# Adding expert results to the tokens' sums on chip, item by item, instead of through DRAM

## What is computed

```python
logits = x2d @ w_router + b_router
top_vals, top_idx = lax.top_k(logits, 4)
gates = softmax(top_vals)
# for each expert e and each token that has chosen it:
gu = xb @ w_gate_up[e] + b_gate_up[e]
g, u = minimum(gu[:, :D_FF], 7), clip(gu[:, D_FF:], -7, 7)
hid = (u + 1.0) * (g * sigmoid(1.702 * g))
out = (hid @ w_down[e] + b_down[e]) * gate
y = zeros((n, D)).at[row_tok].add(out)
x = layer_norm(DEEPNORM_ALPHA * x + y, ln2_g, ln2_b)
```

## Time and profile before

| what | us |
|---|---|
| median of 3 runs | 1552.32 (1551.21 to 1552.47) |
| span of the profiled execution | 1546.4 |
| PE busy | 1282.3 (83%) |
| DVE busy | 347.7 (22%) |
| ACT busy | 260.4 (17%) |
| POOL busy | 70.2 (5%) |
| PE, gate and up (L1536, 2112 instructions) | 478.8 |
| PE, down (L1552, 1056 instructions) | 277.3 |

### The profile page before, as it was taken

How to read it: one execution, slowest core, us unless ns; L and a number is a source line. 1 busy time by engine, 2 the same in 40 slices (tenths; PEclk the granted TensorE clock), 3 DMA queues, 4 the chain that set the end, 5 groups by cost and what they waited for, 6 DMA issues and landing times.

```text
span 1546.4 us, 19222 instructions
## 1 busy us (share of the span) xinstructions
PE 1282.3 (83%) x6721; PEld 512.7 (33%) x6722; DVE 347.7 (22%) x661; ACT 260.4 (17%) x439; POOL 70.2 (5%) x104
## 2 busy tenths in 40 slices
PE   8997787875696989988899888899888878887875
PEld 3444554553444322322223222233222222222222
DVE  0003546465554010012101100100100010001006
ACT  0003556565321011010000000000000000000000
POOL 0000000000000000000000000000000000000003
PEclk9999899996595999989899999999999999999997
DMA  9055898997113999999999999799999999999965
GB/s 388 23 191 175 254 325 299 346 349 309 42 66 146 373 418 418 417 416 418 418 418 416 418 418 419 286 417 416 418 418 418 416 417 418 419 417 416 418 278 170
DMA packets 127322, 526.65 MB, mean 341 GB/s; under 512 B 14720, under 2 KB 14848, under 8 KB 93344
## 3 DMA queue, kind: packets, MB, share of 16 engines
q1 hardware_dynamic: 116080, 496.95, 80.3%
q0 software_dynamic: 5936, 20.71, 4.1%
q10 hardware_dynamic: 5280, 8.65, 1.5%
HBM read 507.39 MB, written 18.87 MB: 340 GB/s over the span
## 4 chain that ended last, share of the span: by engine, by line
PE 32%; DMA 16%; SPq 12%; DVE 5%; issue 2%; ACT 1%; POOL 0%; ACTq 0%; POOLq 0%
DMA arena<-in_w_gate_up 15%; PE psum L1536 15%; PE psum L1552 12%; SPq L225 12%; PE psum L1527 2%; PE psum L1542 1%; DVE arena L1639 1%; DVE arena L1635 1%; DVE arena L1631 1%; DVE arena L1632 1%; ACT arena L1597 1%; PE psum L1572 1%; PE psum L1427 0%; PE psum L1584 0%; SPq L1461 0%
## 5 line engine op out<-in xcount | busy, mean ns | idle before, releaser
L1536 PE MATMUL psum<-arena 128*64 128x512 f32 x2112 | 478.8, 601 | 33.1 <-DMA arena<-in_w_gate_up 33.0
L1552 PE MATMUL psum<-arena 128*64 128x512 f32 x1056 | 277.3, 685 | 22.6 <-ACT arena L1597 22.6
L1536 PEld LDWEIGHTS psum<-arena 128*64 128x64 f32 x2112 | 143.7, 138 | 367.5 <-issue 270.9
L1631 DVE TENSOR_SCALAR arena<-psum 128x512 f32<-128x512 f32 x33 | 22.8, 692 | 864.5 <-PE psum L1536 864.5
L1552 PEld LDWEIGHTS psum<-arena 128*64 128x64 f32 x1056 | 82.6, 157 | 197.6 <-issue 164.5
L1595 ACT ACTIVATE arena<-arena 128x512 f32<-128x512 f32 x33 | 20.8, 630 | 570.9 <-DVE arena L1631 570.9
L599 PE MATMUL psum<-arena 128*128 128x128 f32 x512 | 75.3, 287 | 25.7 <-DMA arena<-in_cache_sb_k 8.2
L1542 PE MATMUL psum<-arena 128*128 128x128 f32 x132 | 25.4, 323 | 74.6 <-DVE arena L1639 74.6
L282 PE MATMUL psum<-arena 128*128 128x512 f32 x192 | 85.8, 603 | 0.0
L506 ACT ACTIVATE arena<-psum 128x512 f32<-128x512 f32 x112 | 61.9, 574 | 82.2 <-PE psum L599 50.1
L599 PEld LDWEIGHTS psum<-arena 128*128 128x128 f32 x512 | 56.3, 144 | 41.3 <-issue 15.0
(11 more groups left out here) (192 smaller groups left out, 856.5 us busy)
## 6 DMA issues: line engine op xcount, KB each, us to landing
arena<-in_w_gate_up SPq DMA_DIRECT2D x256, 1024.0 KB, 20.2
arena<-in_w_down SPq DMA_DIRECT2D x128, 1024.0 KB, 23.2
arena<-in_cache_sb_k SPq DMA_DIRECT2D x64, 256.0 KB, 4.4
arena<-in_cache_diff_k SPq DMA_DIRECT2D x64, 256.0 KB, 8.2
arena<-in_cache_sb_v SPq DMA_DIRECT2D x64, 256.0 KB, 5.1
arena<-in_cache_diff_v SPq DMA_DIRECT2D x64, 256.0 KB, 6.7
arena<-in_w_in SPq DMA_DIRECT2D x8, 1536.0 KB, 20.4
expert_rows<-arena ACTq DMA_DIRECT2D x66, 128.0 KB, 6.1
```

Of the source, the lines that this page charges most:

```text
L1536: ins = nc.tensor.matmul(psum[64 * h:64 * h + 64, n, :], x_k, slot[k][:, col:col + 512], start=False, stop=(k == KD - 1))
L1552: ins = nc.tensor.matmul(psum[64 * h:64 * h + 64, 4, :], h_k, slot[s][:, col:col + 512], start=(k == 0), stop=(k == KD - 1))
L1631: nc.vector.tensor_scalar(gate_in, psum[:, 0, :], LIMIT, None, ALU.min).then_inc(gate_clamped, 1)
```

## The change

The table now gives 2 x token + 2, and 0 for an unused slot. At the end of each item DVE builds `scatter`, a 0/1 matrix of 128 slots (64 twice) by 320 tokens. One item later TensorE multiplies it with `y_rows` (`scatter_rows`: two matmuls for each block, one for each half of 64 rows, into two PSUM banks), and DVE multiplies the result with the item's gate for each token and adds it to `base` (`drain`). `base` starts as DEEP times x1 by three ScalarE copies. `turn(t + 1)` is moved behind the down matmuls, because the drained banks include bank 2. `y_dram`, its stores, its zero fill, the final gathers and the combining matmuls are gone. The first item stands ahead of the loop. The diff, cut to its core:

```diff
-    put("half", i // 64)
+    put("tokens", 2 * np.arange(TOKENS)[None, :] + 2)
+    put("half", i // 64 - 2)
...
-                pool.dma_start(y_dram[EXPERTS * SLOTS:, :].rearrange("(i s) d -> s i d", s=SLOTS),
-                               zeros[0:SLOTS, :].rearrange("p (o d) -> p o d", o=1).to_broadcast([SLOTS, MAX_EXTRA, D])
-                               ).then_inc(rows_zeroed, 16)
...
+                link.mark(nc.vector.tensor_copy(slot_token, psum[:, 2, 0:TABLE_ITEMS]))
...
+        PART = ((5, 6), (7, 2), (0, 1))
...
-                for b in order:
-                    nt = BLOCKS[b][1]
-                    for k in range(TOP_K):
-                        pool.indirect_dma_start(picks[0:nt, 4 * b + k, :], None, y_dram, bass.IndirectOffsetOnAxis(
-                            ap=place_y[0:nt, b, k:k + 1], axis=0)).then_inc(picked_up[b], 16)
...
             def _(pe):
+                def scatter_rows(b):
+                    t0, nt = BLOCKS[b]
+                    for h in range(2):
+                        r = slice(64 * h, 64 * h + 64)
+                        ins = nc.tensor.matmul(psum[0:nt, PART[b][h], :], scatter[r, t0:t0 + nt], y_rows[r, :],
+                                               start=True, stop=True)
+                    ins.then_inc(combined, 1)
...
                     pe.wait_ge(xg_copied, t + 1)
+                    if not first:
+                        pe.wait_ge(drained, 3 * t + (SEED - 3))
                     loaded = pe.value_load(started_i[0:1, bass.ds(t, 1)], min_val=16, max_val=16 * EXPERTS)
...
-                    turn(t + 1)
+                    if not first:
+                        pe.wait_ge(y_copied, t)
+                        pe.wait_ge(scatter_ready, t)
+                        scatter_rows(0)
+                        scatter_rows(1)
                     pe.wait_ge(hid_ready, t + 1)
                     for c in range(4):
                         ins = nc.tensor.transpose(psum[:, 3, c * P:(c + 1) * P], hid[:, c * P:(c + 1) * P], ident)
                     ins.then_inc(hid_turned, 1)
+                    if not first:
+                        scatter_rows(2)
                     pe.wait_ge(hid_copied, t + 1)
...
+                    if not first:
+                        pe.wait_ge(drained, 3 * t + (SEED - 1))
+                    turn(t + 1)
...
+                    pe.wait_ge(base_ready, 6)
+                for b in range(3):
+                    scatter_rows(b)
...
             def _(act):
+                for b in range(3):
+                    nt = BLOCKS[b][1]
+                    nc.scalar.activation(base[0:nt, b, :], x1[0:nt, b, :], ACT.Copy, scale=DEEP).then_inc(base_set, 1)
...
-                    act.wait_ge(y_stored, 32 * t + SEED)
+                    if not first:
+                        act.wait_ge(combined, 3 * t + SEED)
                     nc.scalar.activation(y_rows, psum[:, 4, :], ACT.Copy).then_inc(y_copied, 1)
-                    act.wait_ge(y_copied, t + 1)
-                    for h in range(2):
-                        act.dma_start(y_dram[bass.ds(t * SLOTS, SLOTS), h * 512:(h + 1) * 512],
-                                      y_rows[64 * h:64 * h + 64, :]).then_inc(y_stored, 16)
...
+                def drain(b, col):
+                    nt = BLOCKS[b][1]
+                    banks = PART[b]
+                    at_once = 2 if banks[1] == banks[0] + 1 else 1
+                    for h in range(0, 2, at_once):
+                        r = base[0:nt, b, h * 512:(h + at_once) * 512].rearrange("p (h d) -> p h d", h=at_once)
+                        ins = nc.vector.scalar_tensor_tensor(out=r, in0=psum[0:nt, banks[h]:banks[h] + at_once, :],
+                                                             scalar=item_gate[0:nt, b, col], in1=r,
+                                                             op0=ALU.mult, op1=ALU.add)
+                    return ins
...
                     nc.vector.tensor_tensor(hid, up_in, sig, ALU.mult).then_inc(hid_ready, 1)
+                    if first:
+                        dve.wait_ge(base_set, 3)
+                    else:
+                        for b in range(3):
+                            dve.wait_ge(combined, 3 * t + (b + SEED - 2))
+                            if b == 0:
+                                dve.wait_ge(drained, 3 * t + (SEED - 3))
+                            drain(b, bass.ds(t - 1, 1)).then_inc(drained, 1)
+                    nc.vector.tensor_scalar(scatter, const["tokens"], slot_token[:, bass.ds(t, 1)], None, ALU.is_equal
+                                            ).then_inc(scatter_ready, 1)
                     copy_x(t + 1)
...
-                            link.link(nc.vector.tensor_tensor(r[:, cols_], r[:, cols_], psum[:, COMBINED_BANK[b] + c, :], ALU.add))
...
+                        if c == 0:
+                            dve.wait_ge(combined, 3 * extras + (3 * EXPERTS + b + SEED - 2))
+                            link.link(drain(b, bass.ds(extras + (EXPERTS - 1), 1)))
```

More of the change, by code:

```diff
@@ L81, in constants @@
     put("slot", j % SLOTS)
-    put("token2", 2 * (i + np.array([[b[0] for b in BLOCKS]])))
-    put("half", i // 64)
+    put("token2", 2 * (i + np.array([[b[0] for b in BLOCKS]])) + 2)
+    put("tokens", 2 * np.arange(TOKENS)[None, :] + 2)
+    put("half", i // 64 - 2)
     put("is_c0", c == 0)
@@ L1389, in _ @@
                 dve.wait_ge(table_done, 1)
[L1390 to L1397, removed]
+                link.mark(nc.vector.tensor_scalar(idx_all, psum[:, 2, 0:TABLE_ITEMS], const["half"], 0.0, ALU.add, ALU.max))
+                link.mark(nc.vector.tensor_copy(slot_token, psum[:, 2, 0:TABLE_ITEMS]))
                 dve.wait_ge(col_turned, 1)
@@ L1432, in items @@
             extras = eng.value_load(count_i[0:1, 0:1], min_val=0, max_val=MAX_EXTRA)
+            body(0, first=True)
             if midway is None:
-                with eng.Fori(0, EXPERTS) as t:
+                with eng.Fori(1, EXPERTS) as t:
                     body(t)
             else:
-                with eng.Fori(0, EXPERTS // 4) as t:
+                with eng.Fori(1, EXPERTS // 4) as t:
                     body(t)
@@ L1574, in bias, with body @@
                                              ).then_inc(bias_done, 1)
[L1575 to L1587, removed]
+                    pe.wait_ge(base_ready, 6)
+                extras = items(pe, body, bias)
+                pe.wait_ge(drained, 3 * extras + (3 * EXPERTS + SEED - 3))
+                pe.wait_ge(y_copied, extras + EXPERTS)
+                pe.wait_ge(scatter_ready, extras + EXPERTS)
+                pe.wait_ge(xg_copied, extras + (EXPERTS + 1))
+                for b in range(3):
+                    scatter_rows(b)
             @block.scalar
             def _(act):
-                act.sem_inc(y_stored, SEED)
-                def body(t):
+                for b in range(3):
+                    nt = BLOCKS[b][1]
+                    nc.scalar.activation(base[0:nt, b, :], x1[0:nt, b, :], ACT.Copy, scale=DEEP).then_inc(base_set, 1)
+                def body(t, first=False):
                     act.wait_ge(gate_clamped, t + 1)
@@ L1620, in _ @@
             def _(dve):
+                dve.sem_inc(drained, SEED)
                 nc.vector.memset(ones_row[0:1, :], 1.0).then_inc(ones_ready, 1)
+                link = Count(dve, dve_link)
+                link.n = links[0]
                 def copy_x(t):
@@ L1625, in copy_x, with body @@
                     nc.vector.tensor_copy(xgT, psum[:, 2, :]).then_inc(xg_copied, 1)
-                copy_x(0)
-                def body(t):
+                def drain(b, col):
[8 more added lines that the diff above has]
+                    return ins
+                copy_x(0)
+                for b in order:
+                    nt = BLOCKS[b][1]
+                    link.link(nc.vector.reciprocal(norm_cols[0:nt, 32 + b:33 + b], norm_cols[0:nt, 28 + b:29 + b]))
+                    link.link(nc.vector.tensor_scalar(gates[0:nt, b, :], gates[0:nt, b, :],
+                                                      norm_cols[0:nt, 32 + b:33 + b], None, ALU.mult))
+                    for k in range(TOP_K):
+                        link.mark(nc.vector.tensor_scalar(gate_tmp[0:nt, k, :], const["slot"][0:nt, 0:TABLE_ITEMS],
+                                                          places[0:nt, 1, b, k:k + 1], gates[0:nt, b, k:k + 1],
+                                                          ALU.is_equal, ALU.mult))
+                    link.wait()
+                    link.link(nc.vector.tensor_reduce(item_gate[0:nt, b, :], gate_tmp[0:nt].rearrange("p k i -> p i k"),
+                                                      AX.X, ALU.add))
+                def body(t, first=False):
                     dve.wait_ge(w_used[KD - 1], t + 1)
@@ L1659, in residuals @@
                             link.link(ins)
[L1660 to L1663, removed]
                     dve.sem_inc(weight_ready, 1)
```

(11 more changed lines are left out.)

71 lines of the change are left out of this document (25 added, 46 removed).

## The result

The changed kernel takes 1577.6 us (median of four runs, 1577.1 to 1579.5) against 1551.8 us for the kernel before (four runs): ratio 1.0179, 95% interval 1.0163 to 1.0195 (these two medians alone divide to 1.0167). It is 1.8% slower. The forecast said 3.7% slower, 1610 us, in a range of 1550 to 1635. The direction and the mechanism came out, and the time lies in the range; the size of the loss was over-stated by more than a factor of two. The profiled execution spans 1577.5 us.

What follows compares the result with a forecast made beforehand. Weight loading was taken as the present bound, TensorE as the next at 32.5 us an item. Loop +75, tail -15 and zero fill -2.7 turn span 1546.4 into 1604; plus 5.9 gives 1610 us, range 1550 to 1635.

Steps and rivals of the forecast that it cites:

- the stores' saving: Stores of expert rows in the loop: removing 31 saves 19.4 us, if loading stays the bound.
- the hand-over: From the late turn behind down to the next item's bias: turn, copy and register load add 2.2 us an item.
- The rival with a clock that holds at the hand-over: In the loop, the clock stays full between items: period 29.8 us, 1526 us in all, chance 0.14.
- The tail: From the last down's end to the kernel's end: 42.7 us becomes 27.7, a gain of 15 us.
- midway part beyond an item: The loop's midway part costs about 11 us more than an item, as in the kernel before.
- the clock's price: At bias and early gate/up, the clock falls to half in nearly each item: 2.7 us an item (1.3 to 3.4).
- rival B: In the loop, the clock falls in under half the items or for a shorter time: 1562 us, chance 0.14.
- +0.5 for scatter_rows(2): Behind the transposes of hid, the third block's scatter matmuls outlast ScalarE's copy: 0.5 us an item (0.2 to 1.05).
- rival D: In the scatter matmuls, the two row halves don't overlap: 1.05 us more a period, 1644 us, chance 0.04.
- the 0.5 an item that was weighed: Array shape changes on TensorE's path: three drains might add 0.5 us an item, 16 us in all; taken as 0.
- the zero fill: Fill of 4864 KB beside the page loads: removing it saves one TensorE wait, 2.7 us (0 to 5).
- the 5.9 us between span and median: Whole kernel: the timed median lies 5.9 us above the profiled span, added to the forecast span of 1604.

## Why the prediction was right and wrong

Right: TensorE became the bound and the stores' saving was not to be had; the hand-over cost 2.21 us; the one-row bias did not hold the clock; the row halves overlapped (eight instructions in 1.99 us, which DVE's work on `hid` covers); DVE's drains cost the path nothing; the clock held in down, but for the first item. The rival with a clock that holds at the hand-over forecast 1526 us; made real by the 128-row bias it takes 1513.

```profile
1030.29 1.99 PE L1505 MATMUL psum<-arena 64*128 64x512 f32 x8
```

The tail, down's end to the end of the span, was 1577.5 - 1549.9 = 27.6 us, forecast 27.7:

```profile
1549.91 0.60 PE psum L1497 x4
...
1574.13 0.68 DVE arena L1128
```

Too large was the sum. Its terms, against the profiled execution (span 1604 forecast, 1577.5 measured):

| term | forecast us | measured us | difference |
|---|---|---|---|
| start of the first item's bias | 494.9 | 485.4 | -9.5 |
| first item | 30.4 | 32.2 | +1.8 |
| 32 items, full clock | 32 x 29.8 | 32 x 29.57 | -7.4 |
| 32 items, clock lost | 32 x 2.7 | 32 x 2.17 | -17.0 |
| midway part beyond an item | 11 | 16.7 | +5.7 |
| tail | 27.7 | 27.6 | -0.1 |

The 16.7 are down's end to the next bias at the midway part, 757.0 - 738.1 = 18.9, less the 2.2 of the hand-over, which every item has. The 2.17 are what 32 items take, (1549.9 - 517.6 - 16.7)/32 = 31.74, less the 29.57 of the item at the full clock. The first item has no scatter yet, and its down part met the low clock (8.78 us), which is its +1.8.

The failing step is the clock's price, "I take 2.7 (1.3 to 3.4)", and in it the reason "whose pattern is exactly the new one": the first item's price was taken to hold for nearly every item. In the kernel before, the clock of the first item is low from 498.2 to 505.0, 6.8 us, and that costs 3.4 us. In the changed kernel nine of the 32 items repeat this and lose 3.35 us (19.19 instead of 15.84 for bias and gate/up). One loses nothing, the one behind the midway part 4.3, and the other 21 are at the low clock for 3.4 us only and lose 1.7. The mean is 2.2. The price of 1.7 stood in rival B, "for the shorter time seen". The range had this, the chosen value did not, and with 32 items each tenth counts 3.2 us. In the full clock's period stood +0.5 for scatter_rows(2); the chain shows gate/up's end to down's start at 34.87 - 30.39 = 4.48 instead of 4.16, so +0.3. The stated range also leaves out rival D (1644 us), which the prediction's account of it does not say.

On switching array shapes: scatter_rows(2), 64-row matmuls behind 128-row transposes, takes 1.01 us for four instructions, where overlapped halves at gate/up's pace would take 0.87:

```profile
1033.21 0.66 PE psum L1543 x4
1033.87 1.01 PE psum L1505 x4
```

The Trainium skill, TensorEngine Tiling (Array Packing), Key Properties, says that a change of tiling mode drains TensorE. The trace does not contradict it, but all that it could cost at this place is in these 0.14 us. The undisturbed item, 29.57 us, is the 27.02 of before plus 0.32 here and 2.21 at the hand-over, to within 0.02, so the 0.5 an item that was weighed are not there. One other place, the same in both kernels, may pay: behind a one-row bias gate/up takes 13.91 us at the full clock, behind a 128-row bias 13.75. Whether these 0.16 us come from the change of shape no run isolates.

The second miss is the zero fill: 2.7 taken, range 0 to 5, 12 to 13 measured. The step read the one wait behind the fill and not the eight others of the same kind; all nine take 8.2 us in the kernel before. The first item of the changed kernel begins 12.1 us earlier than before (485.42 instead of 497.57), so some 4 us more came with them:

```profile
485.42 3.28 PE L1524 MATMUL psum<-arena 1*64 1x512 f32 x8 [1.45 <-DVE arena L1631]
```

Third, with the other sign: "the midway part costs about 11 us, as now". Its weights were hidden under down before; moving the turn moved DVE's copy, and with it the weights. I had asked who waits for copy_x in the loop but not at the loop's seam. Last, the 5.9 us between span and median were too much: the median of the changed kernel is 0.1 us above the profiled span. That execution took 1579.5 us in all, 2.0 above its span, so 5.9 held mostly the spread between executions. With it the forecast is 32.4 us too high: 26.5 in the span, of which the clock's price is 17.0, and 5.8 here.

## What to carry to other kernels

When an operation is moved to the seam of a loop, count the whole hand-over there, the sequencer's register loads behind the wait included, and ask what the queue used to run ahead of; here 2.2 us in 32 items and the clock lost with it outweighed 46 us of savings (stores 18, zero fill 13, tail 15). When TensorE has only a few us an item to spare, look at what fills each stretch without wide matmuls: a 2.2 us wait that was moved next to thin matmuls cost 2.2 us of clock on top. A loss seen once is not the loss of each item: look whether it comes in more than one size, and how often each. Where TensorE waits for loads again and again, price a removed transfer by its bytes (11.9 us estimated and 13 measured, 19.4 and 18.0), not by the one wait that follows it.

## What the runs showed that was not expected

Multiplying a bias row with 127 rows of zeros beside it costs no time (1.94 us instead of 1.93) and saved 64 us of 1578, since the clock then stayed at 2.4 GHz through a 2.2 us idle wait in nearly every item. Two one-row matmuls in that wait, with TensorE busy throughout, did not. Two wide ones there saved 57 us.
